# The two softmax maps' logits of prompt attention, from full-height matmuls on a zeroed query to 64-row matmuls on the two halves of the array

## What is computed

```python
logits = jnp.einsum('bqhmd,bkhmd->bhmqk', q, k) * (DA_DH ** -0.5)      # d = 64, m = 0, 1
logits = jnp.where(dist >= 0, logits + bias, -1e30)
p = jax.nn.softmax(logits, axis=-1)
attn = p[:, :, 0] - lam * p[:, :, 1]
o = jnp.einsum('bhqk,bkhv->bqhv', attn, v)
```

## Time and profile before

| | us |
|---|---|
| median of 3 runs | 2002.08 |
| lowest and highest | 2001.04, 2003.43 |
| span of the profiled execution | 1994.6 |
| PE busy in the span | 1665.6 (84%) |
| DVE busy | 730.8 (37%) |
| ACT busy | 454.2 (23%) |
| POOL busy | 266.4 (13%) |

### The profile page before, as it was taken

One profiled execution on the slowest core, in us unless ns is written; L12 is line 12 of the kernel. 1 busy time (PEld: TensorE's weight loads), 2 busy tenths in 40 slices (PEclk: granted clock), 3 DMA queues, 4 the chain that ended last, 5 costly groups with the idle time before them and its releaser, 6 DMA issues. The chain is left out here.

```text
span 1994.6 us, 22007 instructions
## 1 busy us (share of the span) xinstructions
PE 1665.6 (84%) x7402; PEld 1105.3 (55%) x7403; DVE 730.8 (37%) x1498; ACT 454.2 (23%) x1062; POOL 266.4 (13%) x479
## 2 busy tenths in 40 slices
PE   6998989775999999886996999999799059999950
PEld 4565556553555566553444888888587024444420
DVE  4267767674353535351223211121322312212213
ACT  2233332331343333331223111010322001111100
POOL 1001010101222222212130000000000311111112
PEclk8999989886999989997997999999899579999975
DMA  7001200002010100006764411210412838666426
GB/s 211 0 1 55 64 12 11 1 23 82 12 55 1 53 3 23 1 23 199 245 213 138 146 32 33 63 32 1 131 64 85 224 90 309 245 235 250 175 86 218
DMA packets 140800, 191.83 MB, mean 96 GB/s; under 512 B 10375, under 2 KB 107646, under 8 KB 140702
## 3 DMA queue, kind: packets, MB, share of 16 engines
q1 hardware_dynamic: 125022, 137.48, 22.1%
q0 software_dynamic: 15680, 53.10, 7.6%
HBM read 151.86 MB, written 38.69 MB: 96 GB/s over the span
## 5 line engine op out<-in xcount | busy, mean ns | idle before, releaser
L940 PE MATMUL psum<-branch_part,kept 128*128 128x384 f32 (+1 forms) x576 | 202.4, 507 | 1.2 <-DVE branch_part L1170 1.2
L2127 PE MATMUL psum<-moe_part,kept 128*128 x416 | 186.9, 603 | 5.6 <-DVE kept L2195 3.3
L940 PEld LDWEIGHTS psum<-branch_part,kept 128*128 128x128 f32 (+1 forms) x576 | 109.0, 194 | 77.0 <-issue 19.4
L1604 PE MATMUL psum<-split 128*128 128x368 f32 x384 | 133.3, 347 | 0.0
L474 PE MATMUL psum<-kept,branch_part 128*128 128x368 f32 x384 | 124.9, 481 | 10.0 <-PEq L217 5.0
L1598 PE MATMUL psum<-kept,merge_part 128*128 128x368 f32 x384 | 125.6, 481 | 9.0 <-DMA merge_part<-w_da_out 9.0
L2127 PEld LDWEIGHTS psum<-moe_part,kept 128*128 128x128 f32 x416 | 78.4, 193 | 95.9 <-issue 95.9
L479 PE MATMUL psum<-branch_part,kept 128*128 128x512 f32 (+1 forms) x288 | 127.5, 597 | 1.3 <-DVE kept L660 1.3
L1605 PE MATMUL psum<-split 128*128 128x368 f32 x384 | 126.8, 330 | 0.0
L1606 PE MATMUL psum<-split 128*128 128x368 f32 x384 | 126.4, 329 | 0.0
L1653 DVE TENSOR_TENSOR merge_part<-merge_part,psum 128x368 f32<-128x368 f32 x48 | 23.6, 534 | 254.0 <-ACT merge_part L1629 254.0
(11 more groups left out here) (307 smaller groups left out, 2713.2 us busy)
## 6 DMA issues: line engine op xcount, KB each, us to landing
branch_part<-cache_k SPq DMA_DIRECT2D x64, 256.0 KB, 4.9
branch_part<-cache_v POOLq DMA_DIRECT2D x64, 256.0 KB, 5.0
moe_part<-w_gate SPq DMA_DIRECT2D x16, 1024.0 KB
moe_part<-w_up SPq DMA_DIRECT2D x16, 1024.0 KB
moe_part<-w_down SPq DMA_DIRECT2D x16, 1024.0 KB
expert_out<-kept POOLq DMA_DIRECT2D x26, 512.0 KB, 4.1
branch_part<-w_in SPq DMA_DIRECT2D x8, 1024.0 KB, 8.8
merge_part<-w_in SPq DMA_DIRECT2D x16, 512.0 KB
```

What stands on the lines that cost most here:

```text
L940: mm = pe.matmul(bank_of(("z", h, i))[:ROWS[i], 0:384], K["xT"][:, k, cols(i)], Wb[h % 2][:, k, :], start=(k == 0), stop=(k == KC - 1))
L1604: pe.matmul(banks[j], wh[c % 2][:, k, ch], xh[:, k, chunk(n)], start=(k == 0), stop=False)
L2127: mm = pe.matmul(psum[:, 2 + par, :], XT[par][:, k, :], K["GU"][:, bass.ds(KC * b + k, 1), :], start=(k == 0), stop=(k == KC - 1))
```

## The change

The query is stored once, `qT`, scaled, without zeros. The logits of map m are a matmul of 64 rows: partitions 64m to 64m+63 of `qT` against the same partitions of `kT`. The two maps' matmuls alternate piece by piece in one job, and the semaphore `logits` is raised for map 0 and for map 1 after their last matmuls. For block 8 the meta logits (`meta_scores`) stay at full height: there the zeros move to a small copy of the 16 meta keys, `kz[:, m, :]`, made once a head by `place_qk`. GpSimd clears `kz` instead of `qz`, and copies the sample tokens' query in two half-height pieces with drains before them.

```diff
-            slot += [("L", s, 0), ("L", s, 1)] + ([("e", s, 0)] if s % NQ == NQ - 1 else [])
+            slot += [("L", s, 0)] + ([("e", s, 0)] if s % NQ == NQ - 1 else [])
...
-        qz = [sb(2, TOK) for _ in range(2)]
+        qT = [sb(TOK) for _ in range(2)]
+        kz = [sb(2, META) for _ in range(2)]
...
-            def scores(s, m):
+            def scores(s):
                 h, i = s // NQ, s % NQ
-                r = P if i else META
-                q = qz[h % 2][:, m, COL[i]:COL[i] + r]
-                if m == 0:
-                    pe.wait_ge(x_done, NT * h + i + 1)
-                    if s:
-                        pe.wait_ge(exp_done, 2 * s)
-                n = P * i
+                r, n = (P if i else META), P * i
+                half = [slice(64 * m, 64 * m + 64) for m in range(2)]
+                pe.wait_ge(x_done, NT * h + i + 1)
+                if s:
+                    pe.wait_ge(exp_done, 2 * s)
                 for c in range(0, n, 512):
                     w = min(512, n - c)
-                    mm = pe.matmul(lg[m][:r, c:c + w], q, kT[h % 2][:, FIRST + c:FIRST + c + w], start=True, stop=True)
+                    for m in range(2):
+                        mm = pe.matmul(lg[m][:r, c:c + w], qT[h % 2][half[m], COL[i]:COL[i] + r], kT[h % 2][half[m], FIRST + c:FIRST + c + w],
+                                       start=True, stop=True)
+                        if n == SEQ and c + w == n and m == 0:
+                            mm.then_inc(logits, 1)
                 if n < SEQ:
-                    mm = pe.matmul(lg[m][:r, n:n + META], q, kT[h % 2][:, 0:META], start=True, stop=True)
-                    mm.then_inc(logits, 1)
-                elif m == 0:
-                    mm.then_inc(logits, 1)
+                    for m in range(2):
+                        pe.matmul(lg[m][:r, n:n + META], qT[h % 2][half[m], COL[i]:COL[i] + r], kT[h % 2][half[m], 0:META],
+                                  start=True, stop=True).then_inc(logits, 1)
...
-                    mm = pe.matmul(bank_of(("e", s, 0))[:, META * m:META * m + META], qz[h % 2][:, m, cols(i)],
-                                   kT[h % 2][:, 0:META], start=True, stop=True)
+                    mm = pe.matmul(bank_of(("e", s, 0))[:, META * m:META * m + META], qT[h % 2][:, cols(i)], kz[h % 2][:, m, :],
+                                   start=True, stop=True)
...
-                for m in range(2):
-                    rows = slice(64 * m, 64 * m + 64)
-                    act.activation(qz[h % 2][rows, m, cols(i)], bank[rows, 0:r], ACT.Copy, scale=K["vecT"][rows, 18:19])
+                act.activation(qT[h % 2][:, cols(i)], bank[:, 0:r], ACT.Copy, scale=K["vecT"][:, 18:19])
+                if i == 0:
+                    for m in range(2):
+                        rows = slice(64 * m, 64 * m + 64)
+                        act.activation(kz[h % 2][rows, m, :], bank[rows, P:P + META], ACT.Copy)
...
-                pool.memset(qz[h].rearrange("p a b -> p (a b)"), 0.0).then_inc(setup, 1)
+                pool.memset(kz[h].rearrange("p a b -> p (a b)"), 0.0).then_inc(setup, 1)
...
                 for m in range(2):
-                    pool.tensor_copy(K["Qs"][:, DB * h:DB * h + DB, 16 * h + 8 * m:16 * h + 8 * m + 8],
-                                     qz[h % 2][:, m, META:FIRST].rearrange("p (b s) -> p b s", s=DS))
+                    half = slice(64 * m, 64 * m + 64)
+                    pool.drain()
+                    pool.tensor_copy(K["Qs"][half, DB * h:DB * h + DB, 16 * h + 8 * m:16 * h + 8 * m + 8],
+                                     qT[h % 2][half, META:FIRST].rearrange("p (b s) -> p b s", s=DS))
+                pool.drain()
```

More of the change, by code:

```diff
@@ L1012, in _ @@
                 pe.matmul(psum[:, h, 0:ND], relh[0:33, h, :], bucket[0:33], start=True, stop=True).then_inc(bias_made, 1)
-            run = {"z": product, "x": turn_qk, "L": scores, "e": lambda s, _: meta_scores(s), "a": turn_probabilities,
+            run = {"z": product, "x": turn_qk, "L": lambda s, _: scores(s), "e": lambda s, _: meta_scores(s), "a": turn_probabilities,
                    "o": lambda s, _: outputs(s), "g": lambda s, _: turn_output(s)}
@@ L1041, in place_qk @@
                 act.wait_ge(x_turned, n + 1)
+                if i == 0 and h >= 2:
+                    act.wait_ge(saved, h - 1)
                 if n == 0:
                     act.wait_ge(setup, 3)
-                if i == 0 and h >= 2:
-                    act.wait_ge(saved, h - 1)
-                for m in range(2):
-                    rows = slice(64 * m, 64 * m + 64)
-                    act.activation(qz[h % 2][rows, m, cols(i)], bank[rows, 0:r], ACT.Copy, scale=K["vecT"][rows, 18:19])
+                act.activation(qT[h % 2][:, cols(i)], bank[:, 0:r], ACT.Copy, scale=K["vecT"][:, 18:19])
[3 more added lines that the diff above has]
+                        act.activation(kz[h % 2][rows, m, :], bank[rows, P:P + META], ACT.Copy)
                 act.activation(kT[h % 2][:, cols(i)], bank[:, P:P + r], ACT.Copy).then_inc(x_done, 1)
```

## The result

The changed kernel takes 2011.6 us (median of 4 runs, 2008.0 to 2015.1) against 2001.6 for the kernel before on the same chip (4 runs, 1999.8 to 2003.4): ratio 1.0049 [1.0029, 1.0069]. The forecast said 2010. The profiled execution has a span of 2006.0 us against 1994.6.

The account below looks back on a forecast made before the run. PE was taken to wait on DVE's normalise chain, so halved logits gain nothing; 3.6 + 0.6 + 0.4 - 1.4 - 1.0 + 3.1 + 3.0 = +8.3 us, and 1994.6 + 8.3 + 7.5 gave 2010, range 1994 to 2026.

Parts of the forecast that it names:

- The bound: Prompt attention: PE waits in nearly every slot for DVE's normalise, so PE time saved gains 0 on the path.
- Rival A: PE is the bound after all, so the hidden half of the logits counts: 22 us saved, 1980; chance 0.12.
- The overlap: Logits: both maps run side by side on their row halves at 0.84 ns a column; map 0 ready as before.
- rival B: The logits' halves don't overlap, map 0 is late, 25 us in all: 2029; chance 0.10.
- Changes of tile shape: Switching from 128-row passes to 64-row logits: 0.2 us in 18 slots, 3.6 us, plus 0.6 us in the others.
- the order of the passes in i=5: Map 0's 16-column matmul stands behind map 1's passes: 0.1 us in each of four slots, 0.4 us.
- ScalarE's 0: ScalarE's changed ACTIVATEs in place_qk: no effect, as results are read a slot later; if on the path, up to -10 us.
- Slot i=8: Map 0's second maximum no longer waits 0.34 us for the meta logits, four times: -1.4 us.
- The stage's start: Smaller GpSimd memsets free DVE's copy, so the first projection starts sooner, limited by its weights: -1.0 us.
- The clock: PE's longer waits lower the granted clock in the prompt attention: two terms, +3.1 and +3.0 us.
- The first term, i=8: The third head's slot i=8 loses its full clock like the others: +3.1 us, all at 18 to 19 us.
- The second term: Slots i=4 to 7 may fall to 1.2 GHz after longer waits: two of sixteen at 1.5 us, +3.0.

Follow-up runs that it names:

- the filled kernel: The changed kernel with never-read extra matmuls put into PE's waits on normalise: 1986.3 us, ratio 0.9972 to the kernel before.

## Why the prediction was right, point by point

*The bound.* Right. PE stood more and was busy less, and the stage did not get shorter. Rival A was wrong for this kernel.

*The overlap.* Right: 1.83 us instead of 3.38 for two maps; rival B falls. The rule weighed from the Trainium skill, "TensorE: Matmul & The Clock Gate", Part 3, The mechanism, that matmuls start and end in program order, does not hold here between two halves of the rows: with one map behind the other, eight passes run in 1.92 us, as in pairs. The measurement decides; the 2 us that the rule would have added do not show: the slots at equal clock differ by the little that the next point accounts for.

*Changes of tile shape.* The size a slot was right, the sum was not. Map 0's first add stands 0.09 us later behind the logits, and the logits themselves start 0.20 us behind the last pass of `a` instead of 0.11 (576.67 to 576.88): 0.18 a slot, 0.2 forecast. But the 3.6 us are nearly given back by a step that the prediction had at zero: "map 1's half lies wholly beside DVE's work". It did not quite. In the earlier trace rows map 1's last passes end about 580.84 and DVE's second add starts at 580.88, though its first maximum is over at 580.77; after, the second add starts at 580.34, before the first maximum is through (580.43). The second add had itself waited for PE, too briefly to be listed among the large waits. From the first add to `normalise` it is 3.25 us in the earlier trace rows's slot and 3.05 now. The net of both over a slot is +0.14, +0.06, -0.02 and -0.24 us for i=5 to 8, and +0.06 to +0.19 for i=4: about nothing for a head, where the sum had +3.6 +0.6 +0.4 -1.4 = +3.2 over the four heads. What was wrong is therefore not the shape's cost but the other side of it. The 0.1 us for the order of the passes in i=5 is of the size that i=5 stands above i=6 (+0.14 and +0.06). ScalarE's 0 is not contradicted: it is busy 22.9 us less in the 415 us, and no slot at equal clock is shorter by more than the two steps told here.

*Slot i=8.* The wait for the meta logits is gone, as forecast: -1.4 us in the sum. What DVE gained in i=8 was 0.42 us a slot, this wait and the second add together.

*The stage's start.* Right, and for the reason given. L1248 takes 0.42 us (L1241: 3.53), and the first `z` starts at 490.17 instead of 491.66, 1.5 us sooner; it waits for its weights, as expected. More of it then runs at 1.2 GHz: its 32 passes take 12.59 us instead of 11.99. The first logits come at 508.04 instead of 508.93, 0.9 us sooner (0.7 from the last matmul of the stage ahead), where -1.0 was taken:

```profile
482.41 0.42 DVE L1248 COPY branch_part<-branch_part 33x512 f32<-33x512 f32 x1
...
490.17 10.01 PE L941 MATMUL psum<-branch_part,kept 128*80 128x384 f32 x24 [1.74 <-DMA branch_part<-w_in]
```

*The clock.* The step that carries the result, right in kind and too small. The sum had +6.1 us in two terms. The slots have 26.4 us more at 1.2 GHz; at the 0.50 us that the filled kernel gave back for each, that makes 13.2 of their +13.4. The first term, i=8: the third head lost its full clock as forecast, but 1.25 us, not 3.1, and the first two heads gained 2.1 and 2.0, since the longer fall that each had became a shorter one. "18 to 19 us" for each was wrong, 16.6 to 16.9 came; the three together are at -2.9 us. The second term, the clock in i=4 to 7, was the one mis-sized: two slots of sixteen were taken, and i=6 and i=7 fell in each of the first three heads, +10.4 us. Another +4.3 came in i=0 to 3, where falls came and went, and where the prediction had no term. It had bounded its own at 0 to 24 us, since no row of before showed PE standing 1.7 us in such a slot, and then took 3 without a row that spoke for the low end.

*What it would show wrong.* It named a slot i=7 in which `x` starts clearly sooner than 5.65 us behind the logits. It is 5.53: sooner by 0.12, which is the second add, not a faster pass.

So 2010 against 2011.6 agrees better than its terms, and that part is luck. Of the +8.3 us of the sum, the chain had +3.2 and was about +0.2, the start had -1.0 and was -0.7, the clock had +6.1 and was +13.2, and +0.4 came behind the last logits: +13.1 in place of +8.3. The other stages ran 1.7 us shorter in this profile, and the median of the runs stands 5.6 us over the span, where 7.5 were added. Of that distance the later runs show about 2 us for every execution (2007.98 us and a span of 2006.0 for the one profiled after); the rest was that the profiled execution happened to be a quick one. When the changed kernel was run again on another chip it stood some 19 us over the kernel before (1.0096), more than twice the sum.

## What to carry to other kernels

Work taken from an engine that waits in every iteration bought nothing here; on TensorE it can cost, since the wait grows and the clock can fall right behind it, where the engine is on the path again. Before such a cut, move what the engine waits for (here one DVE operation ahead of another, -7 and -26 us of stage), and only then count on the busy time saved. If a wait must stay, matmuls whose results nobody reads can pay for themselves (-24 us of stage in the changed kernel; nothing shown in the kernel before). Judge them by the length of the stage and the time at 1.2 GHz, take a profile of the unchanged kernel on the same chip, and check with repeated timing, since one profile can show some us that are not there.

## What the runs showed of the hardware that was not expected

- A fp32 pass on one half of the rows starts ahead of passes that were issued before it for the other half, up to three passes here (i=8 with one map after the other: 1.92 us for eight passes of 512 columns).
- 64-row passes side by side cost 0.84 ns a column each, as one of full height does; a pass entered behind 128-row passes starts 0.20 us behind the last, not 0.11.
- DVE's copy of 33x512 elements took 0.42 us alone, 1.83 beside one large GpSimd memset and 3.53 beside two that followed each other.
- More TensorE work made the stage 24 us shorter (454.9 to 430.7). What exactly decides the fall of the clock stays open. In the kernel with one map after the other, waits of 0.7 us before `x` stand with no fall in its slots i=7 of the first three heads, and waits of 1.7 us in the changed kernel with one in each. But the length of the wait does not decide alone: the changed kernel's slots i=5 have waits of 1.6 us before `x` and no fall in any head, and when it was run again the third head had the same waits of 1.65 and 1.69 us in i=6 and i=7 without a fall.
